# Attention heads mixed in pairs with the values stationary, in a two-layer hybrid decoder step

## What is computed

```
for l in range(DEPTH):                      # 2 layers
    a_out = mla_prompt(...)                 # 6 heads, causal softmax, values of width 64
    b_out = combine_dilations(...)          # 6 heads, three dilations merged, values of width 64
    c_out = conv_module(...)                # silu(layernorm(depthwise conv))
    xp = xp + jnp.concatenate([a_out, b_out, c_out], axis=-1) @ w_out[l]
    xp = xp + peer_blocked(rmsnorm(xp, norm_ffn[l]), ...)
```

## Time and profile before

| | us |
|---|---|
| median of 3 runs (lowest, highest) | 2066.34 (2064.66, 2067.21) |
| the profiled execution | 2067.32 |
| its span | 2065.4 |

### The profile page before, as it was taken

How to read it: one execution, slowest core, us unless ns; L and a number is a source line. 1 busy time by engine, 2 the same in 40 slices (tenths; PEclk the granted TensorE clock), 3 DMA queues, 4 the chain that set the end, 5 groups by cost and what they waited for, 6 DMA issues and landing times.

```text
span 2065.4 us, 40864 instructions
## 1 busy us (share of the span) xinstructions
PE 2043.7 (99%) x15610; PEld 1805.3 (87%) x15610; DVE 1557.4 (75%) x3543; ACT 1300.2 (63%) x2567; POOL 118.9 (6%) x138
## 2 busy tenths in 40 slices
PE   9999999999999999999999999999999999999998
PEld 7777899999999888788887769999999998887887
DVE  6855789868899776676677466999688997766766
ACT  5466445658888655565564564556688876655654
POOL 2200010000000010100022000000000001101000
PEclk9999999999999999999999999999999999999999
DMA  9453447776666898898763543677766668988886
GB/s 324 145 162 134 162 153 254 248 252 221 208 220 220 282 314 284 302 322 281 248 228 142 171 164 124 200 252 252 241 220 215 214 218 300 317 287 293 267 268 221
DMA packets 137377, 481.78 MB, mean 233 GB/s; under 512 B 25666, under 2 KB 42082, under 8 KB 130768
## 3 DMA queue, kind: packets, MB, share of 16 engines
q1 hardware_dynamic: 124640, 438.45, 63.6%
q0 software_dynamic: 10496, 40.42, 5.6%
q10 hardware_dynamic: 2048, 0.30, 0.1%
HBM read 475.83 MB, written 104.21 MB: 281 GB/s over the span
## 4 chain that ended last, share of the span: by engine, by line
PE 96%; DVE 2%; ACT 1%; DMA 1%; issue 0%; DVEq 0%; ACTq 0%
PE ps L1226 36%; PE ps L1273 33%; PE ps L842 4%; PE ps L930 3%; PE ps L1238 3%; PE ps L1189 2%; PE ps L938 2%; PE ps L1197 2%; PE ps L1193 1%; PE ps L886 1%; PE ps L1153 1%; PE ps L1027 1%; PE ps L1212 1%; PE ps L895 1%; PE ps L1030 1%; DMA big<-in_peer_wq 1%
## 5 line engine op out<-in xcount | busy, mean ns | idle before, releaser
L2220 DVE TENSOR_TENSOR parts<-region,parts 128x1024 fp32r<-128x1024 f32 x512 | 625.7, 1222 | 300.6 <-ACT parts L1548 298.3
L1226 PE MATMUL ps<-tokens_hi,parts 128*128 128x256 f32 x4096 | 760.5, 284 | 0.0
L1548 ACT CAST parts<-region 128x1024 fp32r<-128x1024 f32 x512 | 538.7, 1052 | 271.1 <-PE ps L1273 207.5
L1273 PE MATMUL ps<-parts,parts_hw 128*128 128x512 f32 x3024 | 688.7, 390 | 0.0
L1273 PEld LDWEIGHTS ps<-parts,parts_hw 128*128 128x128 f32 x3024 | 567.0, 188 | 123.8 <-DVE parts_hw L2270 6.9
L1226 PEld LDWEIGHTS ps<-tokens_hi,parts 128*128 128x128 f32 x4096 | 636.9, 188 | 1.0 <-issue 0.6
L1226 PE MATMUL ps<-parts_hw,parts 128*128 128x256 f32 x2048 | 574.1, 280 | 0.0
L1226 PEld LDWEIGHTS ps<-parts_hw,parts 128*128 128x128 f32 x2048 | 386.8, 189 | 0.0
L1594 ACT ACTIVATE big<-ps 128x256 f32<-128x256 f32 (+31 forms) x252 | 131.7, 522 | 146.9 <-PE ps L1226 146.9
L1582 ACT CAST parts_hw<-big 128x256 fp32r<-128x256 f32 x256 | 170.6, 666 | 0.7 <-DVE big L2281 0.7
L1575 ACT ACTIVATE region<-region 128x128 f16<-128x128 f16 x512 | 169.3, 436 | 0.0
(11 more groups left out here) (328 smaller groups left out, 2244.8 us busy)
## 6 DMA issues: line engine op xcount, KB each, us to landing
region<-in_peer_uT SPq DMA_DIRECT2D x256, 512.0 KB, 4.0
region<-in_peer_v SPq DMA_DIRECT2D x256, 512.0 KB, 4.8
out<-in_state_win_k SPq DMA_DIRECT2D x112, 384.0 KB, 4.8
out<-in_state_win_v SPq DMA_DIRECT2D x112, 384.0 KB, 5.0
big<-in_window_keysT SPq DMA_DIRECT2D x16, 576.0 KB, 5.5
big<-in_state_win_v SPq DMA_DIRECT2D x48, 192.0 KB, 4.5
region<-in_w_out SPq DMA_DIRECT2D x4, 2048.0 KB, 9.0
big<-in_peer_wq SPq DMA_DIRECT2D x4, 2048.0 KB, 11.1
```

The lines of the kernel that those rows point to most:

```text
L1226: mm = pe.matmul(ps[:, j % ZB, 0:SEQ], a, hp[b][:, c, :], start=(c == 0 and n == 0), stop=(c == KD - 1 and n == 2))
L1273: mm = pe.matmul(ps[:, 2 * half + t, :], w_t[a][:, 128 * t:128 * t + 128], v_t[b][:, 512 * half:512 * half + 512], start=(j == 0 and n == ...
L1548: act.copy(hi_t[n % HIGHS], rows_t[n % ROWS]).then_inc(high[l], 1)
L2220: dve.tensor_tensor(lo_t[n % ROWS], rows_t[n % ROWS], hi_t[n % HIGHS], ALU.subtract).then_inc(low[l], 1)
```

## The change

It touches the mixer loop and the start of the out-projection.

- The exponents are divided by their sum before they are turned: VectorE's `divide(s - 1)` stands in step s behind the mask and maximum of unit s, and `turn_probs` waits for `prob_ready` in place of `exp_ready`.
- Two heads are mixed together (`mix_values(g)` in steps 3, 5, ... 13, ahead of that step's `turn_probs`), with the values stationary (128x64) and the turned probabilities moving (256 and 128 columns). The two heads write to partitions 0 to 63 and 64 to 127 of one bank, channels on partitions. Six jobs O replace twelve, and the six jobs mT are gone, as is `oAB`. ScalarE casts the high part (`high_heads`), VectorE subtracts for the low part (`low_heads`, waits for the cast), each right after the pair; in `low_heads(0)` VectorE waits for the stores to be done.
- The scores of the dilated heads are made in pairs in steps 6, 8 and 10, alternating the halves of the rows; the second goes to its own bank. VectorE and ScalarE still read them one in each step; before it writes an odd unit VectorE waits for the turn of the unit two before.
- ScalarE casts the first half of the output weights in step 11, ahead of the copies of the mixed windows (ow).
- The first 5 of 8 channel blocks of `out_high(0, 0)` are multiplied in step 12 and those of `out_high(0, 1)` in step 13, ten products each; the rest stays after the convolution's outputs.
- Buffers move with it: high and low parts of the heads to other places, banks of the two early outputs kept apart.

```diff
     for s in range(2 * NH + 2):
-        if s < 2 * NH:
-            jobs.append((("S", s), "V"))
+        jobs += [(("S", u), "V") for u in scored_in(s)]
...
+        if s >= 3 and s % 2:
+            jobs.append((("O", (s - 3) // 2), "V"))
         if 1 <= s <= 2 * NH:
             jobs.append((("PT", s - 1), "A"))
...
-        if s >= 2:
-            jobs.append((("O", s - 2), "V"))
...
-    jobs += [(("mT", g), "V") for g in range(2 * HP)]
     jobs += [(("os",), "V")]
...
+                def dilated_scores(g):
+                    o = [begin("S", NH + 2 * g + n) for n in range(2)]
+                    for i, c0 in ((0, 0), (1, 128)):
+                        K = 128 * (i + 1)
+                        for n in range(2):
+                            r = slice(64 * n, 64 * n + 64)
+                            mm = pe.matmul(o[n][:, c0:c0 + K], qbT[r, g, 128 * i:128 * i + 128], kbT[r, g, 0:K], start=True, stop=True)
+                            if i:
+                                mm.then_inc(product[now[0]], 1)
...
                 def turn_probs(u):
-                    pe.wait_ge(exp_ready, u + 1)
+                    pe.wait_ge(prob_ready, u + 1)
...
-                def mix_values(u):
-                    wait_moved(pe, "PT", u)
...
+                def mix_values(g):
+                    wait_moved(pe, "PT", 2 * g + 1)
...
+                    o = begin("O", g)
+                    for k, (q0, q1, p0) in enumerate(((0, 256, 0), (128, 256, 256))):
+                        for n in range(2):
+                            u = 2 * g + n
+                            v = va[:, k, 64 * u:64 * u + 64] if u < NH else z[:, k, VB + 64 * (u - NH):VB + 64 * (u - NH) + 64]
+                            mm = pe.matmul(o[64 * n:64 * n + 64, q0:q1], v, probT[:, n, p0:p0 + q1 - q0], start=(k == 0), stop=(k == 1),
+                                           skip_group_check=True)
+                    mm.then_inc(product[now[0]], 1)
...
                     if s == WINDOW_MIX + 1:
+                        wait_moved(pe, "O", EARLY - 1)
+                        out_high(0, 0, 0, EARLY)
...
                     if s == WINDOW_MIX + 2:
+                        out_high(0, 1, 0, EARLY)
...
-                wait_moved(pe, "O", 2 * NH - 1)
-                for g in range(2 * HP):
-                    turn("mT", g, parts=[(oAB[:, t, 128 * g:128 * g + 128], 128, 128, 128 * t) for t in range(2)])
...
+                def high_heads(g):
+                    o = arrive(act, "O", g)
+                    act.copy(mix_hi(g), o[:, 0:SEQ]).then_inc(mix_high, 1)
...
                     if s == WINDOW_MIX:
+                        act.wait_ge(product[now[0]], NUM["S", 2 * NH - 1] + 1)
+                        out_weights_high(0)
...
+                def divide(u):
+                    dve.wait_ge(exp_ready, u + 1)
+                    step(dve.reciprocal(rden[:, u, :], den[:, u, :]))
+                    settle()
+                    for i, c0 in ((0, 0), (1, 128)):
+                        pr_ = prob[:, u % 2, c0:c0 + 128 * (i + 1)]
+                        e = dve.tensor_scalar(pr_, pr_, rden[:, u, i:i + 1], None, ALU.mult)
+                    e.then_inc(prob_ready, 1)
+
+                def low_heads(g):
+                    o = read("O", g)
+                    if g == 0:
+                        dve.wait_ge(stored, 1)
+                    dve.wait_ge(mix_high, g + 1)
+                    dve.tensor_tensor(mix_lo(g), o[:, 0:SEQ], mix_hi(g), ALU.subtract).then_inc(moved_v[now[0]], 1)
...
                         o = read("S", s)
+                        if s >= NH and s % 2:
+                            dve.wait_ge(product[now[0]], NUM["PT", s - 2] + 1)
...
+                    if 1 <= s <= 2 * NH:
+                        divide(s - 1)
                     some_taps(TAPS[s] if s < len(TAPS) else 0)
```

More of the change, by code:

```diff
@@ L85, with scored_in @@
 CONV_STEP = (8, 9, 10, 11, 12)
+EARLY = 5
+def scored_in(s):
+    if s < NH:
+        return [s]
+    return [s, s + 1] if s < 2 * NH and s % 2 == 0 else []
 def job_plan():
@@ L1076, in mix_window, with out_high @@
                               skip_group_check=True).then_inc(product[now[0]], 1)
+                def out_high(c, t, k0, k1):
+                    o = begin("xo", c, t) if k0 == 0 else bank("xo", c, t)
+                    for k in range(k0, k1):
+                        pe.wait_ge(wo_high, KD * c + k + 1)
+                        if c == 0 and k == 2 * HP:
+                            wait_moved(pe, "ycT", 1)
+                        for i, part in enumerate((mix_hi(k), mix_lo(k))):
+                            pe.matmul(o[:, 0:512], part[:, 128 * t:128 * t + 128], out_high_part(c, k), start=(k == 0 and i == 0), stop=False,
+                                      skip_group_check=True)
                 for s in range(2 * NH + 2):
-                    if s < 2 * NH:
-                        scores(s)
+                    if s < NH:
+                        latent_scores(s)
+                    elif scored_in(s):
+                        dilated_scores((s - NH) // 2)
                     if s == EXT_STEP:
@@ L1142, in _ @@
                     turn("ycT", c, parts=tokens(yt, 128 * c))
-                wait_moved(pe, "mT", 5)
                 wait_moved(pe, "os")
-                def out_high(c, t):
-                    o = begin("xo", c, t)
-                    for k in range(KD):
-                        pe.wait_ge(wo_high, KD * c + k + 1)
-                        if c == 0 and k == 2 * HP:
-                            wait_moved(pe, "ycT", 1)
-                        for i, part in enumerate((hiT, mix_lo)):
-                            pe.matmul(o[:, 0:512], part[:, k, 128 * t:128 * t + 128], out_high_part(c, k), start=(k == 0 and i == 0), stop=False,
-                                      skip_group_check=True)
+                wait_moved(pe, "O", 2 * HP - 1)
                 def out_low(c, t):
@@ L1158, in out_low @@
                         pe.wait_ge(wo_low, KD * c + k + 1)
[L1159 removed]
+                        mm = pe.matmul(bank("xo", c, t)[:, 0:512], mix_hi(k)[:, 128 * t:128 * t + 128], out_low_part(c, k), start=False,
                                        stop=(k == KD - 1), skip_group_check=True)
@@ L1445, in _, with out_weights_high @@
                     act.copy(va[:, t, :], o[:, 0:384]).then_inc(moved_a[now[0]], 1)
+                def out_weights_high(c):
+                    act.wait_ge(w_ld[now[0]][(5 + c) % 2], 16 * ((5 + c) // 2))
+                    for k in range(KD):
+                        act.copy(out_high_part(c, k), wview(5 + c)[:, k, :]).then_inc(wo_high, 1)
+                def high_heads(g):
+                    o = arrive(act, "O", g)
+                    act.copy(mix_hi(g), o[:, 0:SEQ]).then_inc(mix_high, 1)
                 for s in range(2 * NH + 2):
@@ L1998, in _ @@
                         window_queries()
-                    u = s - 2
-                    if u >= 0:
-                        dve.wait_ge(exp_ready, u + 1)
-                        step(dve.reciprocal(rden[:, u, :], den[:, u, :]))
-                        o = read("O", u)
-                        settle()
-                        dve.tensor_tensor(oAB[:, :, 64 * u:64 * u + 64], o[:, 0:128].rearrange("p (t c) -> p t c", t=2),
-                                          rden[:, u, :].unsqueeze(2).to_broadcast([P, 2, 64]), ALU.mult).then_inc(moved_v[now[0]], 1)
+                    if s >= 3 and s % 2:
+                        low_heads((s - 3) // 2)
                     if s in WINDOW_STEP:
@@ L2024, in _ @@
                         conv_norm()
-                for g in range(2 * HP):
-                    o = read("mT", g)
-                    dve.wait_ge(mix_high, g + 1)
-                    dve.tensor_tensor(mix_lo[:, g, 0:SEQ], o[:, 0:SEQ], hiT[:, g, 0:SEQ], ALU.subtract).then_inc(moved_v[now[0]], 1)
                 o = read("os")
```

72 lines of the change are left out of this document (36 added, 36 removed).

## The result

The changed kernel takes 2093.97 us (median of 4 runs, 2092.71 to 2096.29), against 2066.78 for the kernel before (4 runs) on the same chip: ratio 1.0135, 95% interval 1.012 to 1.015. So it is slower, as forecast, but by 27 us and not by 12; the time lies above the range.

The account below looks back on a forecast made before the run. TensorE, busy 2043.7 of 2065.4 us, was taken as the bound. New waits against saved matmuls gave +7.0 us in layer 1 and, with -2.1 for the clock, +4.9 in layer 0: together +11.9, 2078 us, range 2052 to 2089.

Parts of the forecast that it names:

- step 4: Mixer stage: nothing covers the division before unit 3's turn; begins 0.5 us early, next step starts 1.05 us late.
- turn of unit 10: Steps 10 and 11: division queued behind other VectorE work, TensorE idles some 3.5 us; stage late by 7.7 us.
- past's mix of step 8: Waits some 2 us for the bank of unit 9's scores, read after the samples' convolution; late by 2.9 us.
- early products: Out-projection products, ten each in steps 12 and 13: their gain there is lost as idle time after; layer 1's tail 0.
- a pair of values: Mixing two heads' values on TensorE: 0.75 us a pair, 4.5 us a layer, saving 4.7 us.
- a pair of scores: Two dilated heads' scores on TensorE, alternating row halves: 0.75 us a pair, saving 2.9 us a layer.
- Rival 4: Paired values and scores: column or row groups do not overlap, matmuls are slower; 2089 us; chance 0.04.
- rival 2: Mixer stage: forecast waits plus half clock after new idle stretches, 4 us a layer; 2088 us; chance 0.10.
- granted clock 1.0 throughout layer 0's tail: Sign for the forecast: dense products keep full clock in layer 0's tail, giving back 2.1 us.
- steps 2 and 3: Start of mixer stage: two products leave, one pair comes; 0.5 of 1.1 us remains, next step begins 0.5 us early.
- Rivals 1 and 3: Mixer stage: TensorE's work stays the end, 2050 us, chance 0.24; or both sides balance, 2070 us, chance 0.12.
- rival 1: Mixer stage: TensorE's work stays the end, waits overlaid or below 2 us a layer; 2050 us; chance 0.24.

Follow-up runs that it names:

- e1: The changed kernel without VectorE's division of the probabilities; TensorE turns the exponents directly. 2075.72 us, ratio 1.0047.
- e4: The kernel before with only the division put ahead of the turn, no pairs or other banks. 2087.30 us, ratio 1.0115.
- e10: e4 with VectorE's better order: division first in steps 4, 10 and 11, samples' convolution in step 7, statistics ending step 11. 2073.83 us, ratio 1.0033.
- e5: The changed kernel with VectorE reordered: samples' convolution in step 7, statistics ending step 11, step 4's division before the new tokens' scores. 2081.38 us.
- e7: e6 with the ten early out-projection products each of steps 12 and 13 back behind the convolution. 2064.44 us, ratio 0.9985.
- e2: The changed kernel with useless matmuls put into four of TensorE's new idle times. 2085.84 us, ratio 1.0096.
- e12: e7 with the first pair mixed behind the past's scores of step 3, not ahead of them. 2060.86 us, ratio 0.9972.
- e3: The changed kernel with the twenty early out-projection products back behind the convolution. 2090.06 us, ratio 1.0114.
- e6: e5 with the division ahead of the new scores in steps 4, 10 and 11, and ScalarE's pair cast ahead of the exponent. 2070.81 us, ratio 1.0019.
- e9: e7 with the dilated scores made one head at a time. 2067.23 us, ratio 1.0004.

## Why the forecast was right in sign and short in size

The stage was late by these amounts in layer 1, counted from its own start in either kernel (1115.00 and 1128.05 us):

| at | forecast | measured |
|---|---|---|
| start of step 4 | -0.5 | +0.7 |
| step 5 | +1.05 | +3.45 |
| step 6 | +1.2 | +3.8 |
| step 8 | +1.3 | +4.3 |
| after step 8 | +2.9 | +5.7 |
| scores of unit 10 | +3.5 | +6.65 |
| turn of unit 10 | +7.7 | +10.8 |
| turn of unit 11 | +7.0 | +10.2 |
| convolution's outputs | +8.8 | +12.95 |
| end of the stage | +7.0 | +12.3 |

Layer 0 ended 12.1 late, forecast 4.9. With 0.8 us ahead of the first stage (the drop at 86 to 90 us) and 0.2 elsewhere that is the 25.5 us of the two spans.

**The waits: right in place and in size.** Forecast and measured (layer 0): turn of unit 3, 2.2 and 1.74; past's mix of step 8, 2 and 2.00; turn of unit 9, 1.5 and 1.39; of unit 10, 3.5 and 3.35; convolution, 3 or more and 2.77 (2.54 in layer 1). From step 8 to the turn of unit 11 each increment of the table agrees with the forecast to 0.35 us. e1, e4 and e10 show that the waits before the turns come from the division's place on VectorE, e5 that the one before the past's mix comes from the samples' convolution, and e7 that the convolution's wait comes from the early products.

**The matmuls: right.** Here are a pair of values (147.90 to 148.70, 0.80 us, forecast 0.75) and a pair of scores (138.48 to 139.34, 0.86, forecast 0.75), layer 0:

```profile
138.48 0.93 PE L1025 MATMUL ps<-big 64*128 64x128 f32 x8
139.34 1.96 PE L871 MATMUL ps<-ident,region 128*128 128x128 f32 x16
...
147.90 0.87 PE L1042 MATMUL ps<-region,big 128*64 128x256 f32 x8 [0.59 <-ACT region L1512]
148.70 0.55 PE L871 MATMUL ps<-ident,region 128*128 128x128 f32 x3
```

Two heads' scores cost the time of one (0.85); two heads' values 0.80 us where one took 0.61 to 0.92. Rival 4 is out. The values' price of 0.75 was partly luck: the forecast read the mix of the past in the earlier trace rows as "a quarter of the serial time and some more", but 1.01 us is 0.15 of 16 x 0.42, and the 0.80 measured is less than half of the serial 2.1, so more than the overlap of two heads made it cheap.

**The step that failed: rival 2's price left out of the sum.** The forecast had the clock at full through all of the stage and even gave 2.1 us back in layer 0's tail; half clock after the new idle time was a rival (4 us a layer and the 2.1: 2088) with a chance of 0.10, because no row of before showed idle time of 3 us with a busy array behind. But before did show a drop with no idle time at all: the same sixteen small products, without a wait in front, ran into half clock in layer 0 and not in layer 1:

```profile
182.05 2.44 PE L1124 MATMUL ps<-big 128*128 128x6 f32 x16
...
1206.97 1.95 PE L1124 MATMUL ps<-big 128*128 128x6 f32 x16
```

That was reason to allow for more drops in either tail. The two stages were forecast 11.9 us longer and came out 24.4 longer. Of the 12.5 us between, about 8.6 lie at the places with half clock:

- Step 4 was to lose 1.55 us and lost 2.75 in both layers, with the clock at 0.66 in its window: 2.4.
- From the turn of unit 10 to that of unit 11 layer 0 was to gain 0.7 and lost 0.95, with the clock at 0.57 in its window; layer 1, at full clock, gained 0.6: 1.6.
- From the turn of unit 11 to the end of the stage the forecast was 0 in layer 1 and -2.1 in layer 0; measured were +2.1 and +0.4, with 10.2 us at half clock in each tail: 4.6.

The sign "granted clock 1.0 throughout layer 0's tail" did not come: it was 0.51 from 203 to 213 us. So rival 2's price of some 10 us was about right, and e2 wins back some 6.7 of it (estimated above) while both tails and one other place still drop. In the tails no run shows how much of the 4.6 is the clock's.

**A mis-sized term: steps 2 and 3.** Forecast 0.5 us early at step 4; measured 0.7 late in layer 1 and 0.6 in layer 0: 2.3 us together. The first pair (0.80) stands ahead of step 3's turn, the turned probabilities of the past wait 0.85 us for ScalarE, and the scores no longer cover it. e12, which moves that pair by one place, wins 0.9 us of this back up to the turn of unit 11 (layer 0). From step 5 to step 8 another 0.6 us a layer was short: ahead of the pair, which waits 0.59, the past's mix already waits 1.70 for ScalarE.

**The early products.** Twenty products were to be as good early as late, since the gain ahead comes back as waiting. They were worse, by 3.9 us (e3, of which 2.2 in the stages) to 6.4 (e6 to e7, all of it in the stages by the traces). The forecast had the convolution's outputs 1.8 us later, counted from the turn of unit 11, and the 1.8 won back behind them; in layer 1 they came 2.75 later and 0.65 was won back. The wait falls in the stretch at half clock, and the ten products of each step don't keep the tail's clock up: with them e6's tails have 10.2 and 6.8 us at half clock, without them e7's have 6.8 each.

**Rivals 1 and 3** asked for waits under 2 us a layer, or half of mine. There are nearly 17 us a layer in the changed kernel. In e12, by the same view, they are 5.7, and there the change does win, by 6 us of the 16 that rival 1 promised.

**What stays open.** What takes the clock down in the tails: it comes at or behind the sparse matmuls of the samples' latents in 23 of the 26 tails of the traces (e9's aside), with or without idle time in front, and not in layer 1 of before nor in either layer of e4, where the same matmuls stand. In the steps ahead of the tails every drop in these traces begins in a wait of 1.39 to 3.37 us or at most 1.4 us behind it: three in the changed kernel, one in e2, six in e3, four in e4, two in e5, one in e10; e1 has one behind 1.41 us early in a tail. But only some such waits are followed by one (three of twelve in the changed kernel), and no run shows what decides. So filling the waits is shown to take drops away; which wait will cost one cannot be told ahead. Executions of one kernel differ by 1 to 10 us; in e4 the two ends, 2085.84 and 2096.10 us, have mean clocks of 0.995 and 0.989, so the spread is at least in part of the same kind.

## To carry to other kernels

Before an operation is put on the path between two engines, list what stands ahead of it in its own engine's order at that moment, and put it first where its input is already there: here the same 0.8 us of VectorE's work cost 20.4 us or 6.8 in the kernel before, and 18.3 or about 1 in the changed one. In a stage of small matmuls with new idle stretches, put the clock into the sum as a term with a range, and not only among the rivals: here waits of 1.39 us and more were followed by half clock some of the time, and what that cost lay between nothing and 1.6 us a place ahead of the tails. Work moved ahead of a wait is only worth its place if something else still covers that wait.

## What the runs showed of the hardware

- Half clock came in or just behind waits of 1.39 to 3.37 us, at three of the twelve such waits of the changed kernel, and was gone from those places when they were filled with matmuls (e2). The Trainium skill (TensorE: Matmul & The Clock Gate, HAM oscillation) says that waits for data which are long enough and recur between short bursts of matmuls throw TensorE back to half clock each time, and that a loop arranged to keep it busy avoids that. The traces agree in part: filler won an estimated 6.7 us in e2, but nine of twelve waits were followed by full clock, and the drop of the earlier trace rows has no idle time in front of it.
- Two heads' fp32 scores in the two halves of 64 rows overlap nearly fully: 0.86 us against 0.85 for one. A pair of values in two halves of 64 columns takes 0.80 us; how much of that is overlap no run shows, since the operands changed sides too.
- 23.9 us more at half clock change the mean granted clock only from 0.996 to 0.991. The mean hides what a stage loses; it has to be read in windows.
